# Attention of a hybrid decoder step: sample value products gathered behind heads 2 to 4, and the next turn's first maximum and exponential moved ahead of the turn's output

## The chip, the cores and the metric

The kernel runs on one core of one Trainium2 chip. The metric is device time in microseconds (us) of one execution. The core has five engines that run their own instruction streams and meet only at semaphores: PE (TensorE, matmuls and transposes), DVE (VectorE), ACT (ScalarE), POOL (GpSimd) and SP (SyncE, which here only issues DMAs). PEld is TensorE's loading of weights, which lies beside its matmuls.

## The reference

One inference step of a two-layer decoder for a prompt of 512 tokens and 8 samples of 4 tokens that share all weights. Most of the time goes into four feed-forward blocks and the projections. The change is in the attention of layer 1: eight heads of 64 values in each of three groups of keys (window 128 at stride 1, window 512 at stride 4, window 2048 at stride 16). For each group

```
s = einsum('bqhd,bqkhd->bhqk', q_blk, kg) + bias;  s = where(valid, s, NEG)
lse = logsumexp(s, axis=-1);  p = exp(s - lse);  o = einsum('bhqk,bqkhd->bqhd', p, vg)
...
wts = softmax(stack(lses), axis=0);  o = sum(stack(outs) * wts)   # over the 3 groups
```

which is one softmax over the keys of all three groups. The samples read cached keys and values of each group (DEC_BATCH x up to 2048 rows x 2 x 8 heads x 64); their keys were already used when the stretch around the change begins, their values are read in it.

## The kernel before, in words

All instruction orders are written out by hand, one stream for each engine, and semaphores are counted against constants. `block.tensor` is PE's stream, `block.scalar` ACT's, `block.vector` DVE's, `block.gpsimd` POOL's, `block.sync` SP's.

The prompt's attention runs in four **turns** (`tile(r, ...)`, r = 0 to 3; r = 0 and 3 are written out, 1 and 2 are a hardware loop). A turn has the 128 prompt positions that are equal to r modulo 4, and goes through 8 heads. For a head h of turn r:

- PE: `scores_dilated` and `scores_local` (L1029, L1041, L1044) write 512 scores for each position into `pair0`; they are issued two heads ahead, behind head h - 2, so the scores of heads 0 and 1 of turn r + 1 are issued behind heads 6 and 7 of turn r.
- DVE: `head(r, h)` adds the bias (L2006, L2007), takes the maximum (L2009) and its negative (L2011, semaphore `s_ok`). Behind each odd head, `qk_tile` copies queries and keys of the next turn together (L1944, L1946).
- ACT: `exps(r, h)` takes the exponential with its sum (L1538, semaphore `p_ok`).
- PE: `turn_probs` transposes the probabilities (L1135); it waits for `p_ok` and is the first thing of a head in PE's stream.
- ACT: `turned` copies the transposed ones out of PSUM (L1545, semaphore `pt_ok`).
- PE: `values_dilated` (L1145) and `values_local` (L1154, L1156) multiply by the values; they are issued one head later.

Behind head 7 PE multiplies the samples' part into place (`sample_outputs`, L1124, which waits for DVE's copy L1988 of the samples' sums) and transposes the turn's output (L1186, which waits for DVE's division L2029). ACT copies that out (L1558).

**The samples' value products** run in the same turns, two samples a turn: `sample_values` has 9 tiles of keys for each sample, of two matmuls each (one for each of two samples, L1112, 128x512 values). The first tile waits for the values (`value_in`) of both samples. Two samples' values are loaded by POOL in six DMAs (`load_values`, L2117 to L2119, 4.5 MB), which it issues once the last tile of the two samples before is done (`sv_done`), since there is one buffer for each sample. In the kernel before, the tiles are spread over six heads: 2, 1, 2, 1, 2, 1 tiles behind heads 2 to 7 of turn 0 and behind heads 0 to 5 of turns 1 to 3.

**Ends of the attention.** The value buffers lie on the buffers of streamed weights, so SP loads the next stage's weights (`wo`) only when the last `sv_done` is there. ACT rounds these weights (`round_hi("wo", ...)`, L1233) ahead of the last `turned` of turn 3.

Of the kernel before, what the change touches and what calls it, by code (L numbers as in the profile page):

```python
# [41 lines left out]
HEADS = 8  # L42
# [7 lines left out]
QB = SEQ // P  # L50
# [105 lines left out]
def first_turn(i):  # L156
    return isinstance(i, int) and i == 0
# [26 lines left out]
def build(nc, A, O):  # L184
# [9 lines left out]
    with ctx:  # L194
# [462 lines left out]
        def _(pe):  # L657
# [445 lines left out]
            def sample_values(r, tiles):  # L1103
                for t in tiles:
                    if t == 0:
                        for s in range(2):
                            pe.wait_ge(value_in[s], 48 * r + 48)
                        pe.wait_ge(pb_ok, 2 * r + 2)
                        if not first_turn(r):
                            pe.wait_ge(sv_evac, r)  # L1110
                    for s in range(2):
                        m = nc.tensor.matmul(pd[32 * s:32 * s + 32, 0, :], p_b[s][:, t, :],  # L1112
                                             v_c0[s][:] if t == 0 else v_c[s][:, t - 1, :],
                                             start=t == 0, stop=t == NCK - 1)
                        if t == NCK - 1:
                            m.then_inc(sv_done, 1)
# [41 lines left out]
                m.then_inc(pv_done, 1)  # L1158

            def tile(r, first, last):  # L1160
                lag = 2 if first else 0
                for h in range(HEADS):
                    turn_probs(r, h, first)
                    if h == 1 and first:
                        pe.wait_ge(v_in, 16 * NG)
                    if h:
                        values_dilated(r, h - 1, first)
                    if h + 2 < HEADS:
                        scores_dilated(r, h + 2, first)
                        scores_local(r, h + 2)  # L1170
                    elif not last:
                        scores_dilated(r + 1, h + 2 - HEADS, False)
                        scores_local(r + 1, h + 2 - HEADS)
                    if lag <= h < lag + 6:
                        n = h - lag
                        sample_values(r, range((3 * n + 1) // 2, (3 * n + 4) // 2))
                    if h:
                        values_local(r, h - 1)
                values_dilated(r, HEADS - 1, first)
                values_local(r, HEADS - 1)  # L1180
                sample_outputs(r)
                pe.wait_ge(on_ok, r + 1)
                if not first:
                    pe.wait_ge(ot_ok, r)
                for c in range(GC):
                    m = nc.tensor.transpose(pc[:, 1, c * P:(c + 1) * P], o_n[:, c * P:(c + 1) * P], ident[:])  # L1186
                m.then_inc(on_t, 1)
# [29 lines left out]
        def _(act):  # L1217
# [316 lines left out]
            def exps(r, h, first):  # L1534
                act.wait_ge(s_ok, HEADS * r + h + 1)
                if not (first and h < 2):
                    act.wait_ge(pt_done, HEADS * r + h - 1)
                nc.scalar.activation(p_p[h % 2][:], s_p[h % 2][:], ACT.Exp, bias=a_stat[:, 1, r, h:h + 1],  # L1538
                                     accum_out=a_stat[:, 2, r, h:h + 1]).then_inc(p_ok, 1)

            def turned(r, h, first):
                act.wait_ge(pt_done, HEADS * r + h + 1)
                if not (first and h < 2):
                    act.wait_ge(pv_done, HEADS * r + h - 1)
                nc.scalar.activation(pt_p[h % 2][:], pb[:, h % 2, :], ACT.Copy).then_inc(pt_ok, 1)  # L1545

            def tile(r, first):
                exps(r, 0, first)
                for h in range(HEADS):
                    if isinstance(r, int) and r == QB - 1 and h == HEADS - 1:  # L1550
                        round_hi("wo", 0, 0)
                        round_hi("wo", 1, 0)
                    if h + 1 < HEADS:
                        exps(r, h + 1, first)
                    turned(r, h, first)
                act.wait_ge(on_t, r + 1)
                tokens = ot[:, :, 0:SEQ].rearrange("p c (q r) -> p c q r", r=QB)
                nc.scalar.activation(tokens[:, :, :, r], pc[:, 1, :].rearrange("p (c q) -> p c q", c=GC), ACT.Copy) \  # L1558
                    .then_inc(ot_ok, 1)

            tile(0, True)
            with act.Fori(1, QB - 1) as r:
                tile(r, False)
            tile(QB - 1, False)
            act.wait_ge(ot_ok, QB)
            act.wait_ge(ots_ok, QB)
            for c in range(GC):
# [11 lines left out]
        def _(dve):  # L1579
# [54 lines left out]
            n = NBUCKET + 1  # L1634
# [365 lines left out]
            def head(r, h):  # L2000
                dve.wait_ge(s_done, HEADS * r + h + 1)
                dve.wait_ge(b0_in[h // 4], 64 * (r + 1))
                b = h % 2
                if not (first_turn(r) and h < 2):
                    dve.wait_ge(p_ok, HEADS * r + h - 1)
                nc.vector.tensor_tensor(s_p[b][:, 0:256], pa[:, b, 0:256], b0[:, h, :], ALU.add)  # L2006
                step.add(nc.vector.tensor_tensor(s_p[b][:, 256:512], pa[:, b, 256:512], b12[:, h, :], ALU.add))  # L2007
                dve.wait_ge(dve_step, step.value())
                step.add(nc.vector.reduce_max(a_stat[:, 0, r, h:h + 1], s_p[b][:], axis=AX_X))  # L2009
                dve.wait_ge(dve_step, step.value())  # L2010
                nc.vector.tensor_scalar(a_stat[:, 1, r, h:h + 1], a_stat[:, 0, r, h:h + 1], -1.0, None, ALU.mult) \  # L2011
                    .then_inc(s_ok, 1)

            def tile(r, last):
                for h in range(HEADS):
                    head(r, h)
                    if h % 2 and not last:
                        qk_tile(r + 1, h // 2)
                if last:
                    round_lo("wo", 0, 0)  # L2020
                    round_lo("wo", 1, 0)
                dve.wait_ge(p_ok, HEADS * (r + 1))
                step.add(nc.vector.reciprocal(a_stat[:, 3, r, :], a_stat[:, 2, r, :]))
                dve.wait_ge(dve_step, step.value())
                sample_values(r)
                dve.wait_ge(pv_done, HEADS * (r + 1))
                if not first_turn(r):
                    dve.wait_ge(on_t, r)
                nc.vector.tensor_tensor(o_n[:].rearrange("p (h d) -> p h d", d=DH),  # L2029
                                        pc[:, 0, :].rearrange("p (h d) -> p h d", d=DH),  # L2030
                                        a_stat[:, 3, r, :].unsqueeze(2).to_broadcast([P, HEADS, DH]), ALU.mult) \
                    .then_inc(on_ok, 1)
                sample_outputs(r)
# [184 lines left out]
```

## Time and profile before

| what | us |
|---|---|
| median of 3 runs | 2324.59 |
| lowest, highest | 2322.32, 2328.8 |
| the profiled execution: time | 2325.67 |
| the profiled execution: span from first to last instruction | 2323.9 |
| PE busy | 2213.8 (95%) |
| DVE busy | 931.5 (40%) |
| ACT busy | 679.7 (29%) |
| POOL busy | 249.3 (11%) |

PE is busy for 95% of the span, so an idle moment of PE anywhere is nearly always time lost. The attention turns lie between about 1684 and 1858 us. The "granted clock" is the share of full speed that TensorE was allowed: 1.00 is 2.4 GHz and 0.50 is 1.2 GHz; its mean over the execution is 0.969.

### The profile page before, as it was taken

To read this page: it belongs to the slowest core of one execution; us is meant where nothing else is said; L and a number is where in the kernel's file an instruction comes from. 1 tells how busy PE (TensorE), PEld (TensorE's weight loads), DVE (VectorE), ACT (ScalarE), POOL (GpSimd) and SP (SyncE) were. 2 spreads that over 40 slices of the span, in tenths; PEclk is the share of its full clock that TensorE was granted. 3 is DMA by queue.
4 is the path that set the end of the run, shared out by engine and by line. 5 is a ranking of instruction groups with operands and counts; after the bars stand their busy time and mean duration, and the time that the engine had idled before them with its cause. 6 is when DMAs were issued, how large, how long until landed. Compare 5 with 4: busy or idle time off the path is not lost.

```text
span 2323.9 us, 42264 instructions
## 1 busy us (share of the span) xinstructions
PE 2213.8 (95%) x17383; PEld 2134.7 (92%) x17383; DVE 931.5 (40%) x1328; ACT 679.7 (29%) x1011; POOL 249.3 (11%) x256
## 2 busy tenths in 40 slices
PE   7999999979999999999999999999878889999998
PEld 7999999978999999999999999989745579999997
DVE  3233322685533332443333243377344363333324
ACT  3222222442422221242222224222222343222213
POOL 0000012104000002200000220210010040000122
PEclk9999999989999999999999999999878889999998
DMA  4233332212232333234333324676653322232331
GB/s 133 83 122 117 103 100 83 73 55 72 82 90 81 90 97 93 69 104 132 100 88 96 87 74 159 195 236 215 208 180 106 108 73 77 86 90 86 94 91 59
DMA packets 379214, 249.19 MB, mean 107 GB/s; under 512 B 8182, under 2 KB 360798, under 8 KB 379086
## 3 DMA queue, kind: packets, MB, share of 16 engines
q1 hardware_dynamic: 369031, 209.99, 30.5%
q0 software_dynamic: 10096, 37.94, 4.6%
q8 instruction: 66, 1.08, 0.2%
q14 instruction: 21, 0.17, 0.0%
HBM read 230.63 MB, written 22.35 MB: 109 GB/s over the span
## 4 chain that ended last, share of the span: by engine, by line
PE 84%; DVE 5%; DMA 5%; issue 2%; ACT 2%; SPq 1%; POOL 1%; POOLq 0%; ACTq 0%; DVEq 0%
PE pair L666 69%; PE pair L701 3%; DMA t_w_raw<-in_attn_w_kv 3%; PE pair L838 3%; PE pair L1112 2%; DMA t_cached_v<-in_cache_kv_w 1%; PE pair L1029 1%; PE pair L678 1%; PE pair L1135 1%; DVE t_u_sum L1823 1%; ACT t_w_hi L1233 1%; DVE t_w_lo L1592 1%; PE pair L1145 1%; DVE t_stream L1741 1%; DVE t_work L1733 0%
## 5 line engine op out<-in xcount | busy, mean ns | idle before, releaser
L1592 DVE TENSOR_TENSOR t_w_lo<-t_w_raw,t_w_hi 128x1024 fp32r<-128x1024 f32 (+2 forms) x292 | 407.1, 1394 | 711.1 <-ACT t_w_hi L1233 711.1
L666 PE MATMUL pair<-t_x_hi,t_w_hi 128*128 128x272 f32 x2816 | 587.1, 290 | 10.7 <-DVE t_w_lo L1592 6.1
L666 PE MATMUL pair<-t_x_lo,t_w_hi 128*128 128x272 f32 x2816 | 583.0, 288 | 0.0
L666 PE MATMUL pair<-t_x_hi,t_w_lo 128*128 128x272 f32 x2816 | 582.3, 288 | 0.0
L1233 ACT ACTIVATE t_w_hi<-t_w_raw 128x1024 fp32r<-128x1024 f32 (+2 forms) x292 | 325.1, 1115 | 826.1 <-PE pair L666 789.2
L666 PEld LDWEIGHTS pair<-t_x_hi,t_w_hi 128*128 128x128 f32 x2816 | 441.7, 189 | 11.8 <-DVE t_w_lo L1592 6.3
L666 PEld LDWEIGHTS pair<-t_x_lo,t_w_hi 128*128 128x128 f32 x2816 | 446.4, 189 | 0.0
L666 PEld LDWEIGHTS pair<-t_x_hi,t_w_lo 128*128 128x128 f32 x2816 | 441.9, 189 | 0.0
L666 PE MATMUL pair<-t_h_hi,t_w_hi 128*128 128x272 f32 x1232 | 255.7, 289 | 0.0
L666 PE MATMUL pair<-t_h_lo,t_w_hi 128*128 128x272 f32 x1232 | 254.0, 287 | 0.0
L666 PE MATMUL pair<-t_h_hi,t_w_lo 128*128 128x272 f32 x1232 | 253.7, 287 | 0.0
L2067 POOL TENSOR_TENSOR t_work<-t_work,t_stream 128x544 f32<-128x544 f32 x40 | 55.7, 1392 | 1480.1 <-DVE t_stream L1681 1478.8
L666 PEld LDWEIGHTS pair<-t_h_lo,t_w_hi 128*128 128x128 f32 x1232 | 194.3, 188 | 0.0
L666 PEld LDWEIGHTS pair<-t_h_hi,t_w_hi 128*128 128x128 f32 x1232 | 192.3, 188 | 0.0
L666 PEld LDWEIGHTS pair<-t_h_hi,t_w_lo 128*128 128x128 f32 x1232 | 192.2, 188 | 0.0
L1661 DVE TENSOR_TENSOR t_elementwise<-t_elementwise,pair 128x544 f32<-128x544 f32 x88 | 63.5, 721 | 268.6 <-PE pair L666 262.4
L1284 ACT ACTIVATE t_elementwise<-pair 128x544 f32<-128x544 f32 x88 | 54.9, 624 | 355.5 <-PE pair L666 346.9
L1681 DVE SCALAR_TENSOR_TENSOR t_stream<-pair,t_stream 128x544 f32 (+1 forms) x40 | 29.0, 725 | 182.7 <-PE pair L666 182.7
L2069 POOL TENSOR_TENSOR t_work<-t_work,t_elementwise 128x544 f32<-128x544 f32 x40 | 99.0, 2474 | 0.0
L666 PE MATMUL pair<-t_kv_in_hi,t_w_hi 128*128 128x272 f32 x384 | 82.3, 296 | 0.0
L666 PE MATMUL pair<-t_kv_in_hi,t_w_lo 128*128 128x272 f32 x384 | 80.0, 290 | 0.0
L666 PE MATMUL pair<-t_kv_in_lo,t_w_hi 128*128 128x272 f32 x384 | 79.7, 289 | 0.0
(254 smaller groups left out, 2627.8 us busy)
## 6 DMA issues: line engine op xcount, KB each, us to landing
t_w_raw<-in_ffn_w SPq DMA_DIRECT2D x176, 512.0 KB, 3.8
t_w_raw<-in_ffn_w SPq DMA_DIRECT2D x64, 704.0 KB, 4.5
t_cached<-in_cache_kv_w POOLq DMA_DIRECT2D x16, 1024.0 KB, 8.6
t_cached_v<-in_cache_kv_w POOLq DMA_DIRECT2D x16, 1024.0 KB, 10.9
t_w_raw<-in_attn_w_kv SPq DMA_DIRECT2D x24, 512.0 KB, 7.1
t_w_raw<-in_attn_w_q SPq DMA_DIRECT2D x12, 512.0 KB, 3.8
scratch_bias_rows<-scratch_bias_row SPq DMA_DIRECT2D x12, 384.0 KB
t_w_raw<-in_pool_w_in SPq DMA_DIRECT2D x8, 512.0 KB, 3.9
```

Source lines behind the costliest of these rows:

```text
L666: m = nc.tensor.matmul(out[:, j, 0:HALF], w[:, at + k, :], a(k)[:, j * HALF:(j + 1) * HALF], start=first and k == 0 and n == 0, stop=last ...
L678: return nc.tensor.matmul(out[:, j, 0:HALF], invd[:], a[:, hcols(j)], start=first, stop=not first)
L701: m = nc.tensor.matmul(ps[2 * u + s][:, j, 0:HALF], w[:, k, :], a[:, k, hcols(j)], start=k == 0 and n == 0, stop=k == DC - 1 and n == 2)
L838: m = nc.tensor.matmul(pb[:, j, 0:HALF], w[:, k, :], a[:, KH * s + k, hcols(j)], start=s == 0 and k == 0 and n == 0, stop=s == 1 and k == ...
L1112: m = nc.tensor.matmul(pd[32 * s:32 * s + 32, 0, :], p_b[s][:, t, :], v_c0[s][:] if t == 0 else v_c[s][:, t - 1, :], start=t == 0, stop=t ...
L1233: nc.scalar.activation(whi[s][:, 0:KT[stage], :], raw[s][:, 0:KT[stage], :], ACT.Copy) \
L1284: nc.scalar.activation(split(sg[:]), halves(pc if second(stage, i) else pa), ACT.Silu) \
L1592: nc.vector.tensor_tensor(wlo[s][:, 0:k, :], raw[s][:, 0:k, :], whi[s][:, 0:k, :].bitcast(F32), ALU.subtract).then_inc(lo_made[s], 1)
L1661: nc.vector.tensor_tensor(split(hf[:]), split(sg[:]), halves(pd if second(stage, i) else pb), ALU.mult) \
L1681: nc.vector.scalar_tensor_tensor(out=split(x[:, c, :]), in0=halves(out), scalar=scale, in1=split(x[:, c, :]), op0=ALU.mult, op1=ALU.add) \
L2067: nc.gpsimd.tensor_tensor(accs[:], accs[:], x[:, c, :], ALU.add).then_inc(acc_made, 1)
L2069: nc.gpsimd.tensor_tensor(accq[:], accq[:], sq[:], ALU.add).then_inc(acc_made, 1)
```

## The change

It has three parts, on three engines.

1. PE: the samples' 9 tiles are issued as 3, 3, 3 behind heads 2, 3 and 4 of every turn.
2. ACT: the exponential of head 0 of the next turn is issued ahead of the copy `turned` of head 7, and no longer at the next turn's start.
3. DVE: `head(r + 1, 0)` and `head(r + 1, 1)` are issued behind the last `qk_tile` of turn r, ahead of the reciprocal, the samples' copy and the division that end turn r.

```diff
             def tile(r, first, last):
-                lag = 2 if first else 0
                 for h in range(HEADS):
...
-                    if lag <= h < lag + 6:
-                        n = h - lag
-                        sample_values(r, range((3 * n + 1) // 2, (3 * n + 4) // 2))
+                    if 2 <= h < 5:
+                        sample_values(r, range(3 * (h - 2), 3 * (h - 1)))
                     if h:
                         values_local(r, h - 1)
...
-            def tile(r, first):
-                exps(r, 0, first)
+            def tile(r, first, last=False):
+                if first:
+                    exps(r, 0, first)
                 for h in range(HEADS):
-                    if isinstance(r, int) and r == QB - 1 and h == HEADS - 1:
+                    if last and h == HEADS - 1:
                         round_hi("wo", 0, 0)
                         round_hi("wo", 1, 0)
                     if h + 1 < HEADS:
                         exps(r, h + 1, first)
+                    elif not last:
+                        exps(r + 1, 0, False)
                     turned(r, h, first)
...
-            tile(QB - 1, False)
+            tile(QB - 1, False, True)
...
             def tile(r, last):
                 for h in range(HEADS):
-                    head(r, h)
+                    if h >= 2 or first_turn(r):
+                        head(r, h)
                     if h % 2 and not last:
                         qk_tile(r + 1, h // 2)
+                if not last:
+                    head(r + 1, 0)
+                    head(r + 1, 1)
                 if last:
                     round_lo("wo", 0, 0)
                     round_lo("wo", 1, 0)
```

PE's stream in the loop of turns 1 and 2, as one piece of the difference: the end of head 0 and the start of head 1. L1107 and L1108 are the waits for the two samples' values; `t_history`, `t_cached_v_g` and `t_cached_v` are the value buffers.

```order
 L1041 MATMUL pair<-t_k_feat,t_q_tile 32x128 x2
 L1044 MATMUL pair<-t_k_feat,t_q_tile 32x256 x3
-L1107 ISA
-L1108 ISA
-L1112 MATMUL pair<-t_history,t_work 32x512
-L1112 MATMUL pair<-t_cached_v_g,t_work 32x512
-L1112 MATMUL pair<-t_cached_v,t_work 32x512 x2
 L1131 REGISTER_ALU
 L1135 MATMUL pair<-t_ident,t_p_prompt 128x128 x4
```

The waits and the first two tiles leave this place. They stand, with a third tile, behind head 2's scores, two heads later.

DVE's stream in the loop, before, from the last `qk_tile` to the end of the turn (L2023 reciprocal, L1988 the samples' sums, L2029 the division, L1996 the samples' part):

```order
L1946 COPY t_k_tile<-t_k_feat12 128x128
L2022 REGISTER_ALU
L2023 ISA
L2023 RECIPROCAL t_a_stats<-t_a_stats 128x8
L2024 REGISTER_ALU
L1985 ISA
L1988 COPY t_work<-pair3 64x512
L2029 TENSOR_TENSOR t_o_tok<-pair2,t_a_stats 128x512
...
L1996 TENSOR_TENSOR t_o_feat<-pair3,t_o_feat 64x4x8
...
L2038 COMPARE_AND_BRANCH
```

And of the changed kernel at the same place (lines of the changed file are moved: 1 to 5 further down on DVE, 2 up or 1 down on ACT; L2007, L2008, L2010 and L2012 are a head's sums, maximum and negative):

```order
L1947 COPY t_k_tile<-t_k_feat12 128x128
...
L2007 TENSOR_TENSOR t_s_prompt0<-pair0,t_bias0 128x256
...
L2010 TENSOR_REDUCE t_a_stats<-t_s_prompt0 128x1
...
L2012 TENSOR_SCALAR t_a_stats<-t_a_stats 128x1
...
L2007 TENSOR_TENSOR t_s_prompt1<-pair0,t_bias0 128x256
...
L2012 TENSOR_SCALAR t_a_stats<-t_a_stats 128x1
...
L2028 RECIPROCAL t_a_stats<-t_a_stats 128x8
...
L1989 COPY t_work<-pair3 64x512
L2034 TENSOR_TENSOR t_o_tok<-pair2,t_a_stats 128x512
...
L1997 TENSOR_TENSOR t_o_feat<-pair3,t_o_feat 64x4x8
```

Two heads of the next turn now stand ahead of everything that PE's last two steps of the turn wait for.

ACT's stream at the end of turn 0, before (`t_p_prompt` holds probabilities, `t_pt_prompt` their transposes, the buffer number is the head modulo 2):

```order
L1538 ACTIVATE t_p_prompt1,t_a_stats<-t_s_prompt1,t_a_stats 128x512
L1545 ACTIVATE t_pt_prompt0<-pair1 128x512
L1545 ACTIVATE t_pt_prompt1<-pair1 128x512
L1558 ACTIVATE t_o_feat<-pair2 128x4x128
L1562 UNCONDITIONAL_BRANCH
L1562 ISA
```

and of the changed kernel:

```order
L1536 ACTIVATE t_p_prompt1,t_a_stats<-t_s_prompt1,t_a_stats 128x512
L1543 ACTIVATE t_pt_prompt0<-pair1 128x512
L1536 ACTIVATE t_p_prompt0,t_a_stats<-t_s_prompt0,t_a_stats 128x512
L1543 ACTIVATE t_pt_prompt1<-pair1 128x512
L1559 ACTIVATE t_o_feat<-pair2 128x4x128
```

The third row is the next turn's head 0; it now stands between head 6's and head 7's copies of transposed probabilities. SP's and POOL's streams are the same in both kernels.

## Rows read from the trace of the kernel before

**Rows 1.** The page's first line.

```profile
span 2323.9 us, 42264 instructions
```

**Rows 2.** Chain that ended last: start us, us, what.

```profile
1730.46 11.51 DMA t_cached_v<-in_cache_kv_w
...
1770.43 14.47 DMA t_cached_v<-in_cache_kv_w
```

**Rows 3.** Timeline of PE, turn 1 to 2: start, length, instruction, [idle before].

```profile
1754.37 0.66 PE L1135 MATMUL pair<-t_ident,t_p_prompt 128*128 128x128 f32 x4
...
1757.81 0.66 PE L1135 MATMUL pair<-t_ident,t_p_prompt 128*128 128x128 f32 x4
...
1765.56 0.66 PE L1135 MATMUL pair<-t_ident,t_p_prompt 128*128 128x128 f32 x4
...
1768.12 0.66 PE L1135 MATMUL pair<-t_ident,t_p_prompt 128*128 128x128 f32 x4
...
1771.65 1.06 PE L1124 MATMUL pair<-t_ident,t_work 64*128 64x16 f32 x8
1772.64 0.66 PE L1186 MATMUL pair<-t_ident,t_o_tok 128*128 128x128 f32 x4
1776.79 1.11 PE L1135 MATMUL pair<-t_ident,t_p_prompt 128*128 128x128 f32 x4 [3.49 <-ACT t_p_prompt L1538]
...
1785.24 1.03 PE L1112 MATMUL pair<-t_history,t_work 128*32 128x512 f32 x1 [5.18 <-DMA t_cached_v<-in_cache_kv_w]
```

**Rows 4.** The same view: starts of head 3 of turns 0, 2, 3; product waits.

```profile
1706.97 0.66 PE L1135 MATMUL pair<-t_ident,t_p_prompt 128*128 128x128 f32 x4
...
1742.31 1.03 PE L1112 MATMUL pair<-t_history,t_work 128*32 128x512 f32 x1 [7.57 <-DMA t_cached_v<-in_cache_kv_w]
...
1796.40 0.66 PE L1135 MATMUL pair<-t_ident,t_p_prompt 128*128 128x128 f32 x4
...
1825.79 1.03 PE L1112 MATMUL pair<-t_history,t_work 128*32 128x512 f32 x1 [4.63 <-issue]
...
1837.11 0.66 PE L1135 MATMUL pair<-t_ident,t_p_prompt 128*128 128x128 f32 x4
```

**Rows 5.** The same view: heads 1 and 2 of turn 0.

```profile
1690.45 1.11 PE L1135 MATMUL pair<-t_ident,t_p_prompt 128*128 128x128 f32 x4
...
1695.00 1.12 PE L1135 MATMUL pair<-t_ident,t_p_prompt 128*128 128x128 f32 x4
```

**Rows 6.** Timeline of DVE and ACT, end of turn 1.

```profile
1766.30 0.64 DVE L1944 COPY t_q_tile<-t_q_feat 128x128 f32 x3
...
1767.90 0.68 DVE L1988 COPY t_work<-pair 64x512 f32<-64x512 f32 x1 [0.21 <-DVE t_a_stats L2023]
1771.79 0.69 DVE L2029 TENSOR_TENSOR t_o_tok<-pair,t_a_stats 128x512 f32<-128x512 f32 x1 [3.21 <-PE pair L1156]
...
1773.72 0.42 DVE L2006 TENSOR_TENSOR t_s_prompt<-pair,t_bias 128x256 f32<-128x256 f32 x1 [0.47 <-issue]
...
1775.44 0.15 DVE L2011 TENSOR_SCALAR t_a_stats<-t_a_stats  x1
...
1775.84 0.72 ACT L1538 ACTIVATE t_p_prompt<-t_s_prompt,t_a_stats 128x512 f32<-128x512 f32 x1 [1.34 <-DVE t_a_stats L2011]
```

**Rows 7.** Windows: us, PE PEld DVE ACT POOL busy, PEclk (granted clock), DMA, GB/s.

```profile
1687.00:1699.00 12.00, 11.73 (x76) 8.92 (x76) 6.22 (x20) 4.01 (x11) 3.52 (x14) 0.50 1.00 366
1768.00:1771.00 3.00, 3.00 (x51) 2.41 (x41) 0.58 (x1) 0.60 (x1) 2.71 (x9) 1.00 0.96 247
1812.00:1815.00 3.00, 3.00 (x53) 2.50 (x46) 0.81 (x2) 0.00 (x0) 1.66 (x7) 1.00 1.01 305
1815.00:1818.00 3.00, 0.45 (x5) 0.22 (x3) 2.85 (x9) 1.90 (x3) 0.00 (x0) 0.63 1.05 335
```

**Rows 8.** Timeline of POOL: first load of the third pair's values.

```profile
1766.05 0.55 POOL L2117 DMA_DIRECT2D t_history<-in_cache_kv_w  x1 [34.09 <-PE pair L1112]
```

**Rows 9.** Timeline, end of turn 3: ACT's rounding, PE's last products and output.

```profile
1852.63 0.63 ACT L1233 ACTIVATE t_w_hi<-t_w_raw 128x512 fp32r<-128x512 f32 x1 [0.66 <-DMA t_w_raw<-in_attn_w_o]
...
1853.80 1.12 PE L1145 MATMUL pair<-t_v_prompt,t_pt_prompt 128*128 128x64 f32 x4 [2.54 <-ACT t_pt_prompt L1545]
...
1857.27 1.11 PE L1186 MATMUL pair<-t_ident,t_o_tok 128*128 128x128 f32 x4
```

## The prediction

> **What bounds the kernel now.** I read the chain that ended last first: its only long pieces inside the attention turns that aren't PE's are two waits for cached values, 11.51 and 14.47 us from the issue of the last load to its landing [rows 2]. Then the timeline of PE for what it does around them. At full clock a head without a sample tile takes 1768.12 - 1765.56 = 2.56 us, one with one tile 1757.81 - 1754.37 = 3.44 us, so a tile costs 0.88 us [rows 3]. A turn without any idle time at full clock would be 8 x 2.56 = 20.5 us of heads (head 0 has no values of a head before it, but head 7's close the turn), 9 x 0.88 = 7.9 of tiles, 1.0 for L1124 and 0.7 for L1186: **30.1 us**. From head 3 to the next turn's head 3 it really takes 1796.40 - 1754.37 = 42.0 and 1837.11 - 1796.40 = 40.7 us, and 47.4 us from turn 0 to 1, of which 2.6 go to three tiles more than nine [rows 3, 4]. The excess is 14.7 + 11.9 + 10.6 = **37.2 us** over three turn ends.
>
> It has three parts, best seen from turn 1 to 2. PE ends the output's transposes at 1773.3 and idles 3.49 us for the next turn's first exponential; does head 0; idles 5.18 us for the values (7.57 and 4.63 at the other ends) [rows 3, 4]. And it is at half clock in between: the granted clock was 1.00 in 1812 to 1815 and 0.63 in 1815 to 1818 [rows 7], and the first L1135 after the wait takes 1.11 us instead of 0.66 [rows 3].
>
> **The sample tiles (PE).** The last tile moves from behind head 5 to behind head 4 (from head 7 in turn 0), and the first from behind head 0 to behind head 2. No tile is added. POOL issued the load at 1766.05 and it had landed by 1770.43 + 14.47 = 1784.90: 18.9 us [rows 2, 8]. From the last tile to the next turn's first, PE now has heads 5, 6, 7, the turn's end, heads 0 and 1 and most of head 2: 7.7 + 4.5 + 2.0 + 2.6 + 2.2 = 19 us at full clock, and some 24 if heads 0 to 2 are at half clock. I take the wait as 0; its bounds are 0 and 2 us for each turn end (SP's bias loads, issued around head 7, share the DMA engines).
>
> **The first maximum and exponential (DVE, ACT).** The 3.49 us of idle go, since the next turn's head 0 is ready when the output is turned. But both are put ahead of things PE waits for, so a shorter wait takes their place. I count from the start of head 7's transposes on PE. DVE's work for a head takes 1775.44 + 0.15 - 1773.72 = 1.87 us, the copies of queries and keys 1.1, the exponential starts 0.25 us after the negative and its successor follows 0.8 us later [rows 6].
> - ACT: DVE starts head 7 at -2.8, ends it at -0.9 and its copies at 0.2, and the next turn's head 0 at 2.1. The exponential ends at 3.1, and only then head 7's probabilities are copied, until 3.7. PE is ready for them at 2.56: idle 1.1. PE's last products (0.95) end at 4.65.
> - DVE: the scores of the next head 1 are there at 2.3 plus the wait above's share, its maximum at 4.2 to 4.4, then the reciprocal (0.2) and the samples' copy (0.68) [rows 6]: L1124 starts at 5.3, idle 0.6. The division (0.69) is hidden behind L1124. The output is turned at 7.0.
> Queued behind the moved exponential on ACT is only that copy; behind the two moved heads on DVE the copy and the division, and PE alone waits for those. Together 1.7 us. Five heads in a row without tiles now run only as fast as scores, maximum, exponential and transposes follow each other, 5.3 us for two heads (1.87 + 0.25 + 0.8 and 0.6 for the copy [rows 6], 1.7 on PE from L1145 to the end of the next scores, 0.1 between them) against 5.12 of PE's work; about 0.1 us each, 0.5. And 0.3 for ACT's output copy (L1558), which now stands between exponentials 0 and 1. **2.5 us** a turn end, with bounds of 1 (all of ACT's and DVE's share hidden but for the copy) and 3.5 (what the old wait was).
>
> **The clock.** This is the term that decides. At the end of turn 2 the clock was still at 2.4 GHz in 1812 to 1815, with PE shown busy for all of it, and it fell to 1.2 GHz in the next 3 us, though PE had only just run out of work, with the tiny L1124 and the transposes as its last work [rows 7]. The first L1135 behind turn 1 (1.11 us) and the last L1186 of turn 3 (1.11) are at half speed too [rows 3, 9]. The new turn end has the same small instructions, and 1.7 us of idle between them; I expect the clock to fall there again. What brings it back is worse: in turn 0 PE was busy for 11.73 of 12 us with heads that had no tiles, all at 0.50 [rows 7], and L1135 is back from 1.12 to 0.66 us only behind the first dense sample tiles [rows 4, 5]. Those now come two heads later. A head at half clock takes 1695.00 - 1690.45 = 4.55 us [rows 5], 2.0 more than 2.56. So heads 0 and 1 and the part of head 2 ahead of its tiles lose 1.3 + 2.0 + 1.8, and the tiles between 0 and 2.6 (all three at half clock), taken in the middle as 1.3: **6.4 us** a turn end. Bounds: 0 if the clock doesn't fall, 8 if it rises only after the tiles.
>
> The Trainium skill speaks against this term (TensorE: Matmul & The Clock Gate, section Why this matters for your kernels): it keeps full speed as long as no long idle gap opens between bursts of matmuls. By that rule the new turn end, whose gaps are about 1 us, would cost no clock, and the sum below would be about 21 us better. The trace doesn't agree: at 1815 to 1818 the clock fell right at the end of the work [rows 7].
>
> **The last turn.** Its tiles end behind head 4, so SP asks for the output weights 3.4 us earlier in PE's order, and the wait of 2.54 us (ACT's roundings end at 1853.3, ahead of the copy that PE waits for) [rows 9] shrinks. But head 5's tile was also cover: without it head 7 waits about 1 us for its exponential, and 1.0 us of the wait for the rounding stays. The end runs at half clock either way (L1186 took 1.11 us) [rows 9]. Gain **0.5 us**, bounds -1 and 4.
>
> **The sum.** Of 37.2 us, 3 x (2.5 + 6.4) = 26.7 stay: 10.5 gained, 11.0 with the last turn. The profiled execution had a span of 2323.9 and a time of 2325.67 us, 1.1 above the median of 2324.59 [rows 1]. Against its own time: 2325.67 - 11.0 = 2314.7; against the median 2313.6. I say **2313.5 us**. Work outside the attention isn't touched; its length doesn't depend on when the attention ends, but for which moment the clock falls and rises.
>
> **Rivals.**
> 1. *The clock falls at each turn end and comes back only with the tiles* (my forecast), 0.60; its own range is 2308 to 2318.
> 2. *The clock holds over all turn ends.* For it: the idle pieces are only 1.1 and 0.6 us, and 1768 to 1771 held 1.00 without a tile [rows 7]. Against: 1815 to 1818 [rows 7]. Then 3 x 2.5 stay, and the last turn gains about 2.5: 37.2 - 7.5 + 2.5 = 32 us, 2292. This is also where the skill's rule ends. 0.11. Between the two, one or two turn ends hold it: 2299 to 2307, 0.14.
> 3. *The load isn't hidden.* Values land 2 us or more too late three times over, or DVE's turn end costs what the old wait did; PE idles behind head 2 in place of head 0: 2313.5 + 6, about 2319. For it: 18.9 us of load against 19 at full clock. Against: at half clock there are 24. 0.10.
> 4. *Slower: the clock falls behind head 4.* Five heads without tiles follow each other, where before there were at most two, and three of them had tiles to keep the array busy. If heads without tiles can't hold 2.4 GHz, heads 5 to 7 lose 3 x 2.0 us in each of three turns and some 4 in the last, 22 us, less 2 of waits that this hides: 2313.5 + 20 = about 2333. It decides once more than five or six heads in all run at half clock that did not before, 11 us at 2.0 each. Against it: 1768 to 1771, at 1.00 with no tile in it [rows 7]. 0.05.
> That the change doesn't do what it says is no case: all three moves stand in the order of instructions.
>
> **Range and chances.** 0.3% (7 us, below 2317.6) is about what a measurement of this kernel can tell from no change. Faster by more: cases 1 and 2 nearly whole, 0.86. Within 0.3%: case 3 and the edge of case 1, 0.09. Slower: 0.05. The range of 2299 to 2321 leaves out all clocks holding (0.11) and case 4 (0.05).
>
> **What the changed profile would show.** Right: no wait for t_cached_v on PE behind head 0 and none over 1 us behind head 2; L1135 of a turn's head 0 directly behind L1186; idle of about 1.1 us before the last L1145 and 0.6 before L1124 of a turn; from turn to turn some 39 us; a granted clock near 0.5 in heads 0 and 1 and 1.00 by head 3. Wrong: a clock of 1.00 through a turn end (then a turn takes 33 us and the time is nearer 2292), or 0.5 already in heads 5 to 7, or a wait of several us for the values behind head 2.

## The result, and the profile after the change

The changed kernel takes **2311.34 us** (median of 5 runs, 2309.85 to 2313.18) against 2324.59 us for the kernel before in the same rounds (5 runs). The ratio is 0.994 with a 95% interval of 0.9919 to 0.9961: faster by 13 us, by more than the 0.3% that such a measurement can tell from no change. The forecast was 2313.5 us.

The page of the profiled execution (2313.18 us) begins with its span:

```profile
span 2311.4 us, 42264 instructions
```

The number of instructions is the same as in [rows 1]; the span is 12.5 us shorter. All of it is gained between the end of the attention's first turn and the start of the stage behind the output projection. The timeline of PE in the changed kernel (start, length, instruction, idle time before it and what ended it) has the rows that answer to [rows 3] and [rows 4]; L1184 is the line that was L1186:

```profile
1708.33 0.66 PE L1135 MATMUL pair<-t_ident,t_p_prompt 128*128 128x128 f32 x4
...
1730.13 0.60 PE L1135 MATMUL pair<-t_ident,t_p_prompt 128*128 128x128 f32 x4
...
1732.44 1.12 PE L1135 MATMUL pair<-t_ident,t_p_prompt 128*128 128x128 f32 x4
...
1745.79 0.66 PE L1135 MATMUL pair<-t_ident,t_p_prompt 128*128 128x128 f32 x4
...
1764.78 0.71 PE L1145 MATMUL pair<-t_v_prompt,t_pt_prompt 128*128 x4 [0.63 <-ACT t_pt_prompt L1543]
...
1766.91 1.89 PE L1124 MATMUL pair<-t_ident,t_work 64*128 64x16 f32 x8 [0.82 <-DVE t_work L1989]
1768.73 1.12 PE L1184 MATMUL pair<-t_ident,t_o_tok 128*128 128x128 f32 x4
1769.64 0.64 PE L1135 MATMUL pair<-t_ident,t_p_prompt 128*128 128x128 f32 x2
...
1777.35 1.12 PE L1135 MATMUL pair<-t_ident,t_p_prompt 128*128 128x128 f32 x4
...
1781.31 1.06 PE L1112 MATMUL pair<-t_history,t_work 128*32 128x512 f32 x1
...
1786.45 0.66 PE L1135 MATMUL pair<-t_ident,t_p_prompt 128*128 128x128 f32 x4
...
1827.25 0.66 PE L1135 MATMUL pair<-t_ident,t_p_prompt 128*128 128x128 f32 x4
```

The rows 1708.33, 1745.79, 1786.45 and 1827.25 are the starts of head 3 in the four turns: the turns take 37.5, 40.7 and 40.8 us. No wait for `t_cached_v` is left at a turn's end; the sample tiles start at 1781.31 with no idle time before them. (PE's wait ahead of the first turn's tiles, 4.23 us before and 4.09 us now, stays: the change doesn't touch that load.) The next turn's head 0 stands right behind L1184, so the wait of 3.49 us is gone too, and the two new ones (0.63 before the last L1145, 0.82 before L1124) are there instead. The heads from 1769.64 to the tiles run at half clock.

Windows on PE in the same execution (us; PE busy, with its instructions; granted clock; share of the DMA engines; GB/s), which answer to [rows 7]:

```profile
1721.00:1724.00 3.00, 3.00 (x52) 1.00 0.94 318
1728.00:1731.00 3.00, 2.35 (x19) 1.00 1.03 337
1731.00:1740.00 9.00, 9.00 (x66) 0.51 0.59 189
1759.00:1762.00 3.00, 2.96 (x41) 1.00 0.94 341
1762.00:1765.00 3.00, 2.37 (x35) 1.00 1.02 379
1765.00:1768.00 3.00, 2.17 (x23) 0.54 1.01 340
1771.00:1780.00 9.00, 9.00 (x62) 0.50 0.26 84
1787.00:1796.00 9.00, 9.00 (x79) 1.00 0.00 0
```

The clock is at its upper level (2.4 GHz) from the end of head 2's tiles to head 7, at its lower level (1.2 GHz) from a turn's end into the next turn's tiles, and there PE is busy without a gap: 9.00 of 9 us. At the end of turn 0 the fall comes after the output's transposes (1.00 in 1728 to 1731), at the end of turn 1 already with head 7's last products (0.54 in 1765 to 1768), which is why L1124 took 1.89 us there and only 1.06 us one turn earlier.

The end of the last turn, PE's timeline, answers to [rows 9]; L666 is the first matmul of the output projection:

```profile
1842.46 0.66 PE L1135 MATMUL pair<-t_ident,t_p_prompt 128*128 128x128 f32 x4 [0.90 <-ACT t_p_prompt L1536]
...
1844.46 0.66 PE L1145 MATMUL pair<-t_v_prompt,t_pt_prompt 128*128 128x64 f32 x4 [0.49 <-ACT t_pt_prompt L1543]
...
1846.61 0.66 PE L1184 MATMUL pair<-t_ident,t_o_tok 128*128 128x128 f32 x4
...
1849.96 0.79 PE L666 MATMUL pair<-t_o_hi,t_w_hi 128*128 128x272 f32 x2 [2.70 <-DVE t_o_lo L2050]
```

All of it runs at full clock now (0.66 us where [rows 9] have 1.12 and 1.11). Two windows of the changed kernel show how the projection begins:

```profile
1850.00:1854.00 4.00, 4.00 (x18) 0.50 0.00 0
1854.00:1856.00 2.00, 2.00 (x18) 1.00 0.00 0
```

and the timeline and one window of PE in the kernel before show the same place there:

```profile
1861.07 0.79 PE L666 MATMUL pair<-t_o_hi,t_w_hi 128*128 128x272 f32 x2 [2.69 <-DVE t_o_lo L2045]
...
1861.00:1867.00 6.00, 5.93 (x26) 0.50 0.00 0
```

From its first matmul on, the projection has 4 us at half clock instead of 6. **Where the time came from**, by the starts of head 3 and of L666: the first turn's tiles start 0.5 us later than they should by the count (the starts in the profiles below scatter over 4 us, so this is no effect of the edit); the end of turn 0 gives 7.3 us (47.4 less 2.6 for three tiles more, against 37.5), the end of turn 1 1.4 (42.0 to 40.7), the end of turn 2 nothing (40.7 and 40.8), the last turn 3.0 (head 3 to L666 was 23.96 us with four tiles in it, and is 22.71 with six: 23.96 + 1.76 - 22.71), together 11.1. In the last turn 1.15 us of the 3.0 are waits (2.54 before, 0.90 + 0.49 now) and some 1.8 the clock: from the last L1145 to the end of the output's transposes 4.6 us before, 2.8 now. Behind it come 1.35 us more, both pieces at a moment when the clock was low: 0.75 in the projection (its first 24 products on the chain took 5.79 us and take 5.07) and 0.6 in the next stage's first sums (eight matmuls, 3.44 and 2.89 us).

### The profile page after: what moved, and what is told of

It reads as the page before. It is cut to its first block, busy times and chain, and to the rows that moved or that the text cites. A ratio compares the mean times of both kernels' runs of the same rounds, so it can differ in the third digit from the quotient of the medians.

```text
span 2311.4 us, 42264 instructions
## 1 busy us (share of the span) xinstructions
PE 2222.7 (96%) x17383; PEld 2140.6 (93%) x17383; DVE 931.0 (40%) x1328; ACT 679.0 (29%) x1011; POOL 249.4 (11%) x256
## 4 chain that ended last, share of the span: by engine, by line
PE 85%; DVE 6%; DMA 4%; issue 2%; ACT 2%; SPq 1%; POOL 1%; ACTq 0%; POOLq 0%; DVEq 0%
PE pair L666 69%; PE pair L701 4%; DMA t_w_raw<-in_attn_w_kv 3%; PE pair L838 3%; PE pair L1112 2%; PE pair L1029 1%; PE pair L1135 1%; PE pair L678 1%; ACT t_w_hi L1231 1%; DVE t_w_lo L1593 1%; DVE t_u_sum L1824 1%; PE pair L1041 1%; PE pair L1145 1%; DVE t_stream L1742 1%; DVE t_work L1734 0%
## 5 line engine op out<-in xcount | busy, mean ns | idle before, releaser
L666 PE MATMUL pair<-t_x_hi,t_w_hi 128*128 128x272 f32 x2816 | 587.7, 290 | 11.9 <-DVE t_w_lo L1593 6.1
L666 PE MATMUL pair<-t_x_lo,t_w_hi 128*128 128x272 f32 x2816 | 583.0, 288 | 0.0
L666 PE MATMUL pair<-t_x_hi,t_w_lo 128*128 128x272 f32 x2816 | 582.2, 288 | 0.0
L666 PEld LDWEIGHTS pair<-t_x_hi,t_w_hi 128*128 128x128 f32 x2816 | 442.1, 189 | 13.1 <-issue 6.8
L666 PEld LDWEIGHTS pair<-t_x_lo,t_w_hi 128*128 128x128 f32 x2816 | 446.7, 189 | 0.0
L666 PEld LDWEIGHTS pair<-t_x_hi,t_w_lo 128*128 128x128 f32 x2816 | 441.7, 188 | 0.0
L666 PE MATMUL pair<-t_h_hi,t_w_hi 128*128 128x272 f32 x1232 | 255.7, 289 | 0.0
L666 PE MATMUL pair<-t_h_lo,t_w_hi 128*128 128x272 f32 x1232 | 254.0, 287 | 0.0
L666 PE MATMUL pair<-t_h_hi,t_w_lo 128*128 128x272 f32 x1232 | 253.8, 287 | 0.0
L666 PEld LDWEIGHTS pair<-t_h_lo,t_w_hi 128*128 128x128 f32 x1232 | 194.3, 188 | 0.0
L666 PEld LDWEIGHTS pair<-t_h_hi,t_w_hi 128*128 128x128 f32 x1232 | 192.3, 188 | 0.0
L666 PEld LDWEIGHTS pair<-t_h_hi,t_w_lo 128*128 128x128 f32 x1232 | 192.2, 188 | 0.0
L666 PE MATMUL pair<-t_kv_in_hi,t_w_hi 128*128 128x272 f32 x384 | 82.1, 295 | 0.0
L666 PE MATMUL pair<-t_kv_in_hi,t_w_lo 128*128 128x272 f32 x384 | 79.6, 289 | 0.0
L666 PE MATMUL pair<-t_kv_in_lo,t_w_hi 128*128 128x272 f32 x384 | 79.5, 288 | 0.0
## 6 DMA issues: line engine op xcount, KB each, us to landing
t_cached_v<-in_cache_kv_w POOLq DMA_DIRECT2D x16, 1024.0 KB, 10.6
```

What stands on the lines that cost most here:

```text
L666: m = nc.tensor.matmul(out[:, j, 0:HALF], w[:, at + k, :], a(k)[:, j * HALF:(j + 1) * HALF], start=first and k == 0 and n == 0, stop=last ...
```

## The experiments

My theory, as in the prediction: the values' load hides behind the longer stretch without tiles, the waits at a turn's end shrink to small ones, and the clock's fall at each end takes back most of what could be had. The rivals: the moved maximum and exponential do most of it; the clock isn't a term at all, and turns are 40 us long for another reason (latencies between the engines in heads without tiles). Kernels of one group shared a chip and the rounds of the kernel before, and each ratio is to that; medians of different groups are compared only roughly.

**The two halves of the change, each alone.** The first kernel is the one before with only PE's edit:

```diff
-                lag = 2 if first else 0
...
-                    if lag <= h < lag + 6:
-                        n = h - lag
-                        sample_values(r, range((3 * n + 1) // 2, (3 * n + 4) // 2))
+                    if 2 <= h < 5:
+                        sample_values(r, range(3 * (h - 2), 3 * (h - 1)))
```

> The sample tiles behind heads 2 to 4, maxima and exponentials where they were in the kernel before. My theory: the wait for the values is gone, and with it most of the gain; the idle time of about 3 us for the next turn's first exponential is back at three turn ends in place of some 1.6 us of new idle time, the clock falls as it does in the changed kernel: 2311.3 + 3 x 1.4 = about 2315.5 us. Rival: the tiles bring nothing without the other part, since PE then only waits elsewhere: about 2324 us.

Measured: 2315.88 us (8 runs) against 2327.02, ratio 0.9946 (0.9925 to 0.9968). In its timeline of PE no wait for the values is left at a turn's end, and those for the first exponential stand as they were (2.96, 3.49 and 2.55 us; this is the middle one):

```profile
1772.12 1.11 PE L1135 MATMUL pair<-t_ident,t_p_prompt 128*128 128x128 f32 x4 [3.49 <-ACT t_p_prompt L1536]
```

The second is the changed kernel with this edit taken back, so with the moved maxima and exponential alone.

> The first maxima and exponential ahead of the turn's output, the sample tiles where they were before (first behind head 0, last behind head 5). My theory: PE comes to the first tile some 3 us earlier and waits so much longer for values that land when they did: 2324 us, between 2322 and 2326. Rival: the removed wait of about 3 us counts by itself at three turn ends: about 2316 us.

Measured: 2331.39 us (12 runs), ratio 1.0007 (0.9989 to 1.0025): no change that can be told. (The median lies above the range I gave in us; the kernel before took 2327.02 in these rounds.) Its timelines of PE and POOL at the end of turn 0:

```profile
1727.05 0.60 PE L1135 MATMUL pair<-t_ident,t_p_prompt 128*128 128x128 f32 x4
...
1740.91 1.03 PE L1112 MATMUL pair<-t_history,t_work 128*32 128x512 f32 x1 [12.05 <-DMA t_cached_v<-in_cache_kv_w]
...
1724.63 0.55 POOL L2124 DMA_DIRECT2D t_history<-in_cache_kv_w  x1 [34.31 <-PE pair L1112]
```

Head 0 begins with no idle time before it, and PE then waits 12.05 us for values whose loads were issued from 1724.63 on; in [rows 4] the wait was 7.57. At the next ends it is 5.92 and 5.14 instead of 5.18 and 4.63. In all, 9.0 us of waiting for the first exponential went (2.96, 3.49 and 2.55), 5.7 came back as longer waits for the values, and 3.9 as the small new waits ahead of L1145 and L1124 (0.40 at the first end, 1.73 at each of the others). Only the first end shows the take-over nearly pure: 2.96 us removed, 4.5 us more in front of the tiles, 0.40 new. The idle time removed ahead of a wait that ends by itself was worth nothing here, and the tiles carry the change. What the moves add once the tiles are placed is not told apart by times (ratios 0.9946 and, below, 0.9934, with overlapping intervals); the two profiled spans differ by 2313.7 - 2311.4 = 2.3 us, within the scatter of the runs.

**The clock.** The third kernel adds to the changed one dense matmuls whose result nothing reads, one ahead of head 7's last products, one ahead of L1124, one ahead of the output's transposes, in turns 0 to 2:

```diff
+            def filler(n):
+                for _ in range(n):
+                    nc.tensor.matmul(pc[:, 1, :], ident[:], v_p[0][:, 0, :], start=True, stop=True)
...
+                if not first:
+                    pe.wait_ge(ot_ok, r)
+                filler(1 if not last else 0)
                 values_dilated(r, HEADS - 1, first)
                 values_local(r, HEADS - 1)
+                filler(1 if not last else 0)
                 sample_outputs(r)
+                filler(1 if not last else 0)
                 pe.wait_ge(on_ok, r + 1)
-                if not first:
-                    pe.wait_ge(ot_ok, r)
```

> The changed kernel with three useless dense matmuls (128x512, some 0.85 us each at full clock, result overwritten) at each of the four turn ends: ahead of head 7's products, ahead of L1124 and behind it. The first two lie in idle time of 0.3 to 0.9 us. My theory, that the clock falls because the turn end has too little array work and that this costs about 6 us a turn end: the granted clock stays at 1.00 through the three inner turn ends, a turn takes 33 to 35 us, the time is about 2297 us (between 2292 and 2303). Rival, that the clock falls there whatever PE does, or costs little: 2311.3 plus up to 4 us.

Measured: **2296.21 us** (6 runs), ratio 0.9864 (0.9839 to 0.9889): nine matmuls more, and 15 us less than the changed kernel's 2311.34 of other rounds (by the ratios 18). Its timeline of PE at the end of turn 1 (L1162 is the filler; each is two records that overlap, about 1 us in all), and then its windows over the three ends:

```profile
1756.78 1.13 PE L1162 MATMUL pair<-t_v_prompt,t_ident 128*128 128x512 f32 x2
...
1758.60 1.13 PE L1162 MATMUL pair<-t_v_prompt,t_ident 128*128 128x512 f32 x2
1759.65 1.06 PE L1124 MATMUL pair<-t_ident,t_work 64*128 64x16 f32 x8
1760.64 1.12 PE L1162 MATMUL pair<-t_v_prompt,t_ident 128*128 128x512 f32 x2
...
1762.04 0.60 PE L1135 MATMUL pair<-t_ident,t_p_prompt 128*128 128x128 f32 x4
```

```profile
1722.00:1731.00 9.00, 8.91 (x86) 1.00 1.04 346
1755.00:1767.00 12.00, 11.66 (x121) 1.00 0.92 315
1790.00:1800.00 10.00, 9.82 (x99) 1.00 0.99 336
```

The granted clock stays at 1.00 from 1703 to 1823, over all three ends, and the turns take 33.6, 33.9 and 33.4 us. Of that 30.1 are the turn by the prediction's count (30.5 by the rows, as the part on the prediction shows) and some 2.9 the three fillers, so at full clock there is hardly anything else in a turn, and the heads without tiles are not limited by latency.

The fillers also stand where PE was idle, so they might only keep order. The next kernel puts three of them where the clock is high and PE has work anyway, behind head 5, in each turn:

```diff
+                    if h == 5:
+                        if not first:
+                            pe.wait_ge(ot_ok, r)
+                        filler(3)
```

> Control: the same three fillers of e3 behind head 5 of each turn, in the middle of dense work, none at the turn end. If the place at the turn end is what makes them pay, the clock falls as in the changed kernel and they only cost 4 x 2.6 us, less what they hide of the exponentials' waits: about 2320 us. If e3 gained for another reason (any more dense work, a later turn end), it is near e3's 2296 us.

Measured: 2321.44 us (12 runs), ratio 0.9975 (0.9958 to 0.9991): 10 us slower than the changed kernel (of other rounds; 8 by the ratios), about what its twelve matmuls cost. Its timeline and windows of PE at the end of turn 1:

```profile
1769.49 0.65 PE L1145 MATMUL pair<-t_v_prompt,t_pt_prompt 128*128 x4 [0.99 <-ACT t_pt_prompt L1551]
...
1771.26 1.89 PE L1124 MATMUL pair<-t_ident,t_work 64*128 64x16 f32 x8 [0.74 <-DVE t_work L1997]
...
1767.00:1770.00 3.00, 2.01 (x32) 1.00 1.04 346
1771.00:1780.00 9.00, 8.74 (x42) 0.50 0.48 155
```

The clock falls at the turn's end as before; the place of the dense work counts, not its amount.

**Idle time or light work?** This kernel has no fillers; it is the changed one with the moved pieces placed where they hold up neither the last products nor L1124:

```diff
-                    elif not last:
-                        exps(r + 1, 0, False)
                     turned(r, h, first)
+                if not last:
+                    exps(r + 1, 0, False)
...
                 if not last:
                     head(r + 1, 0)
-                    head(r + 1, 1)
...
                     .then_inc(on_ok, 1)
+                if not last:
+                    head(r + 1, 1)
                 sample_outputs(r)
```

> The changed kernel with the next turn's first exponential behind head 7's copy of transposed probabilities, and the next turn's maximum of head 1 behind the division: PE then finds its last products and L1124 ready, and head 1's exponential is still in time. My theory: some 1.4 us of idle time goes at each of three turn ends, and the clock falls all the same, since what is left there (small products, L1124, transposes) is light work: 2311.3 - 4 = about 2307 us. Rival, that the clock falls because of the idle time: it stays at 1.00 and the time is about 2290 us.

Measured: **2296.76 us** (6 runs), ratio 0.9859 (0.9833 to 0.9884). I had expected the clock to fall at every end all the same; in the profiled execution it did so at one of three. That execution took 2300.71 us and was the slowest of the six, so the others may have lost less. Its windows of PE:

```profile
1722.00:1726.00 4.00, 4.00 (x61) 1.00 1.03 375
1727.00:1740.00 13.00, 13.00 (x81) 0.50 0.65 206
1760.00:1770.00 10.00, 9.23 (x117) 1.00 1.03 352
1771.00:1777.00 6.00, 6.00 (x29) 0.50 0.38 110
1795.00:1807.00 12.00, 11.18 (x138) 1.00 0.98 333
1808.00:1811.00 3.00, 3.00 (x9) 0.50 0.00 0
```

At the end of turn 0 it fell at 1726.1, with PE busy for all of the 4 us before: the work there was head 7's last products, the transposes and L1124 with its 16 columns. At the ends of turns 1 and 2 it held, and fell later: at 1770.5 with the start of the next turn's head 2, for whose exponential PE had just waited 0.79 us (and 0.34 for head 1's), and at 1808.0 at the tiles, where PE had just idled 1.39 us. The row names no releaser; the DMA engines had been busy with the values until about 1807:

```profile
1797.96 1.06 PE L1124 MATMUL pair<-t_ident,t_work 64*128 64x16 f32 x8
1798.96 0.66 PE L1184 MATMUL pair<-t_ident,t_o_tok 128*128 128x128 f32 x4
...
1807.80 0.85 PE L1112 MATMUL pair<-t_history,t_work 128*32 128x512 f32 x1 [1.39 <-issue]
```

Then the turns take 37.7, 34.9 and 33.8 us. Taking away 1.2 to 1.5 us of idle time an end, 4.2 in all, gave 15 us against 2311.34 (19 by the ratios), more than three times that idle time; the rest is clock. So the idle time counts, and since the clock fell once with no idle time before it, it is not all that counts. That the lightness of the work is the other part is my reading of these windows; the kernels with fillers at the same places, below, bear on it.

**How little is enough.** Five kernels with fewer fillers. With the places of the kernel just shown and one filler on either side of L1124 in every turn:

> e4 with two of the useless dense matmuls at each turn end, ahead of L1124 and behind it. In e4 the clock still fell at the end of turn 0 and in head 1 and 2 of later turns, and the wait for values came back once (1.39 us). My theory: with dense work in the turn end the clock stays at 1.00 through the three inner ends; a turn takes 30.1 + 1.7 + 0.5 = 32.3 us, to which a wait for the values of 0 to 1.5 us may come, since the load takes 19 us: about 2293 us (2289 to 2297). Rival, that without idle time the fillers only cost: 2296.8 + 6.8 (4 x 1.7) = 2303 us.

2294.69 us (4 runs), ratio 0.9862 (0.9846 to 0.9879). The same with the tiles behind heads 2 and 3 alone, so that the load is asked for a head earlier:

```diff
-                    if 2 <= h < 5:
-                        sample_values(r, range(3 * (h - 2), 3 * (h - 1)))
+                    if 2 <= h < 4:
+                        sample_values(r, range(5 * (h - 2), 5 + 4 * (h - 2)))
```

> e5 with the samples' nine tiles as 5 and 4 behind heads 2 and 3, so that each load starts one head (2.6 us) earlier. My theory: what is left of the wait for the values goes and nothing else changes: e5 less 0 to 4 us, about 2291. Rival, that six heads in a row without tiles let the clock fall: 5 us or more slower than e5.

2296.31 us (5 runs), ratio 0.9865 (0.9844 to 0.9885). In neither does PE wait for values at a turn's end, and the clock is 1.00 from 1705 to 1821 in both; a load asked for earlier had nothing to win. Next, the changed kernel with two fillers a turn, ahead of head 7's products and ahead of L1124:

> The changed kernel with only the two fillers that lie in its idle time (ahead of head 7's products and ahead of L1124), none behind L1124; the waits of the moved maxima and exponential are kept. If idle time in which the array works keeps the clock, this costs almost nothing and holds it: turn 32.9 us, about 2293 us. If the third filler of e3 was needed, the clock falls at one or more of the three ends and the time lies between 2298 and 2308 us.

2292.41 us (4 runs), ratio 0.9857 (0.984 to 0.9874). Without the last turn's two, in the next rounds:

> e7 without its two fillers in the last turn, whose end is followed by 2.7 us of idle time and the output projection whatever they do (from head 3 of the last turn to the first product of the projection 23.9 us in e7, 23.1 in e4 without fillers): e7's 2292.4 less 1 to 2 us, about 2291. Rival, that they also pay there: slower than e7 by 1 us or more.

2291.25 us (4 runs), ratio 0.9845 (0.9822 to 0.9868). At full clock the load shows again, once, in the timeline of PE of the first of these two:

```profile
1735.92 0.59 PE L1112 MATMUL pair<-t_history,t_work 128*32 128x512 f32 x1 [1.16 <-DMA t_cached_v<-in_cache_kv_w]
```

And the places that hold up nothing, with one filler ahead of L1124 in turns 0 to 2:

```diff
                 values_local(r, HEADS - 1)
+                filler(0 if last else 1)
                 sample_outputs(r)
```

> e4 with one dense filler (0.85 us) ahead of L1124 at the three inner turn ends only. If little more array work is enough to hold the clock once the idle time is gone: a turn of 30.1 + 0.9 + 0.5 = 31.5 us, to which 1 to 1.5 us of waiting for the values come since the load takes 19 us; about 2290 us. If not, the clock falls at one or more ends, or behind a wait for values, and it stays near e4's 2296.8.

**2290.24 us** (5 runs) against 2328.01, ratio 0.9852 (0.9831 to 0.9873). Its windows of PE over the three ends:

```profile
1719.00:1727.00 8.00, 7.94 (x94) 1.00 1.03 359
1751.00:1760.00 9.00, 8.79 (x104) 1.00 1.03 353
1783.00:1792.00 9.00, 8.96 (x108) 1.00 1.02 365
```

In this execution, the fastest of the five, three matmuls of 1 us hold the clock from 1703 to 1822; the turns take 32.2, 33.2 and 31.6 us. What the three add to the kernel without fillers the times don't tell: the ratios are 0.9852 and 0.9859 with nearly the same intervals. The mean granted clock of the runs is 0.975 to 0.980 with them and 0.970 to 0.977 without. The changed kernel once more, in the same rounds:

> The changed kernel as it is, on the chip and in the rounds of e9 and e10, so that they can be compared: 2311 us (2308 to 2314), and the clock low from the end of each turn to head 2 of the next.

2311.23 us (6 runs), ratio 0.9934 (0.9917 to 0.9952). So both this version and the one with two fillers at each inner end beat the changed kernel by 20 us in the same rounds, with intervals that don't meet; between the two the runs don't tell.

## Why the prediction was right

- **The sample tiles.** Right. No wait for the values was left in the changed kernel at any end, and the tiles alone give nearly the whole gain (0.9946 against 0.994). The margin is not as small as I made it: in the changed kernel the DMA engines ran out at 1736.5, 1774.5 and 1815.5, which is 4.5 to 7 us ahead of the tiles, about what the half clock costs the heads in between. With the clock held it is about 2 us in the kernel with nine fillers, and PE waited for the load once or twice, 0.3 to 1.4 us, in three of the other kernels, as the rival of the load not hidden had it, for far less than its 2 us an end.
- **The moved maxima and exponential.** The places and sizes of the new waits were right (1.1 and 0.6 us said; 0.26, 0.63, 0.84 and 0.95, 0.82, 0.67 measured), 1.2 to 1.5 us an end. Of the 0.8 that I added for heads without tiles and for ACT's copy in front of exponential 1, some 0.4 shows at the ends of turns 1 and 2: heads 6 and 7 take 2.68 and 2.80 us (1758.67 to 1764.78, less the wait of 0.63) for 2.56, at full clock. The first wait in turn 0 was shorter than I worked out from the end of turn 1.
- **The clock.** The term that I called the one that decides was the right one: with the clock held, the changed kernel's turns take 32.5 to 33.9 us with two fillers of 1 us in them, against 37.5 to 40.8. Its size was off for the ends of turns 1 and 2. The durations say 0.8 us for L1124, 0.5 for L1184, 0.8 for head 0, 2.0 for head 1 and 3.9 for head 2 with its tiles (1777.35 to 1786.45, 9.1 us, against 2.56 + 2.64), 8.0 in all where the sum had 6.4. I let the clock fall behind the output's transposes, at 1.3 us lost in head 0; it fell ahead of L1124. At the end of turn 0 it did fall where I had it, the heads lost 2.0 + 3.6 us, and the end kept 7.4 us of excess in place of 8.9. At the other two it kept 10.6 and 10.7. The 1.1 us by which the first of these is more than its waits (1.45) and the 8.0 lie in the rows too: 0.3 in head 7's products, already at half clock (1.31 us for 0.97), 0.4 in the heads 6 and 7 just named, and 0.4 in the count of 30.1, which is low: by rows at full clock head 0 takes 2.31, the last products 0.97 and L1184 0.49 us, which makes a turn without idle time 30.5.
- **The last turn.** Mis-sized: 3.0 us instead of 0.5. The step that failed is "the end runs at half clock either way": the clock held at 1.00 until 1847.2, L1135 to L1184 took 0.66 us each, and that was worth some 1.8 us. The wait for the rounding, said to be 1.0, was 0.49. The kernel with the tiles alone has the same 22.71 us from head 3 to L666, so this belongs to the tiles. The wait before head 7's exponential (0.90) was said (about 1).
- **Outside the attention** I said that nothing changes but the moments when the clock falls and rises. That exception was worth 1.35 us, 0.75 in the output projection and 0.6 at the start of the next stage; I had given it no price.
- **The sum.** By the turns' ends 5.8 + 3.0 + 1.7 and 0.5 for the last turn were said, 11.0; measured are 7.3, 1.4, -0.1 and 3.0, then 1.35 and the 0.5 us of the start the other way: 12.5. The total is nearer than its parts: two ends were put too high, one end and the last turn too low, and these cancel by luck.
- **Rival 2, the clock holds.** Priced at 2292, it was wrong for this kernel and right as a price: with the clock held by six extra matmuls the changed kernel takes 2291. The Trainium skill's rule that I weighed (TensorE: Matmul & The Clock Gate, section Why this matters for your kernels) asks for no long idle gaps between bursts. No gap of the changed kernel's turn ends is over 0.95 us, and the clock fell at each; in the kernel with no fillers it fell once with no gap at all in the 4 us before. So gaps alone don't decide it here.
- **Rival 4, the clock falls behind head 4.** It did not: the clock was 1.00 in 1759 to 1765, through heads 5 to 7. The kernel with the tiles as 5 and 4 shows more: six heads in a row without tiles, at 1.00 throughout. In turns 1 and 2 of the changed kernel, though, the clock fell within the last products of head 7, earlier than I had it.

**Left open.** What makes the clock hold at one turn end and fall at the next with the same instructions (the kernel without fillers: fell at the end of turn 0, held at those of 1 and 2) is not settled by these runs; and whether the moment at which an end comes plays a part was not tried. The runs show that fillers in the idle places hold it, and that without the idle time it falls less often. Each kernel's clock was read in one execution. The single matmul an end of the version at 2290 may thus be near an edge.

## What to carry to other kernels

Before a wait is shortened, ask which later wait ends by itself: here 9.0 us of idle time removed in front of three loads came back as 5.7 us more of waiting for them and 3.9 of new small waits, and only placing the load's consumer two heads later made room. Then read the granted clock beside every place where the array runs out of dense work, since the stretch of heads behind it at half clock costs more than the idle time; six useless matmuls at such places bought 20 us, twelve of them behind head 5, where PE had work anyway, cost 10. And once the clock holds, loads that the slow stretch used to hide can come back as waits, here of 0.3 to 1.4 us.

## What the runs showed of the hardware

- At half clock, PE stayed there through 9.00 us of 9 without a gap, with transposes and products of 64 to 256 columns as its work (1771 to 1780), and came back at 1785.8, during the 512-column tiles that began at 1781.3. Busy time alone doesn't bring the clock back here.
- The stretches at half clock from the end of turn 0 on were 13.7, 20.5, 20.5 and 6.8 us long in the changed kernel, and 17.1, 13.7, 13.6 and 13.7 us in the one before. Turns with the same products thus differ by up to 3.3 us in time (37.5 and 40.8), which no instruction explains, and the moment of the fall moved the last turn by some 1.8 us. At the end of turn 2 the waits shrank by 5.7 us (2.55 + 4.63 to 0.84 + 0.67) and the turn took as long as before: PE worked through nearly all of its 20.5 us at half clock, where before it had idled for half of the 13.6.
- Twelve dense matmuls behind head 5 cost 10 us; nine at the turn ends gave 15, and six of them, in the idle places alone, 20.
